# One Trainium2 core, two transformer blocks: input projection with gate and rope pairs in turn, rope and weight sums on VectorE, new order of products and of the attention steps

## What is computed

```python
q, k, v, u, b, c, ga, gc = split(hx @ w_in)     # 1024+256+256+1024+1024+1024+1024+1024 columns
q, k = rope(q, cos, sin), rope(k, cos, sin)     # x*cos + rotate_half(x)*sin
y = b * conv3(c * u)                            # three taps along the tokens
o = window_attention(q, k, v, k_ctx, v_ctx, sink)   # 16 heads of 64, 4 key heads, 128-token query blocks
x = x + g1 * ((sigmoid(ga) * (o @ w_proj_attn) + sigmoid(gc) * (y @ w_proj_conv)) @ w_out)
```

## Time and profile before

| | us |
|---|---|
| median of 3 runs (2946.32 to 2947.89) | 2946.53 |
| the profiled execution | 2949.81 |
| its span, first to last instruction | 2948.0 |
| TensorE busy in it | 2778.3 |
| VectorE busy in it | 2023.5 |

### The profile page before, as it was taken

One profiled execution on the slowest core, in us unless ns is written; L12 is line 12 of the kernel. 1 busy time (PEld: TensorE's weight loads), 2 busy tenths in 40 slices (PEclk: granted clock), 3 DMA queues, 4 the chain that ended last, 5 costly groups with the idle time before them and its releaser, 6 DMA issues.

```text
span 2948.0 us, 35284 instructions
## 1 busy us (share of the span) xinstructions
PE 2778.3 (94%) x13692; PEld 2208.9 (75%) x13692; DVE 2023.5 (69%) x2811; ACT 1303.2 (44%) x2017; POOL 724.1 (25%) x607
## 2 busy tenths in 40 slices
PE   7999999999999999898999989999999489999997
PEld 6777777888778778777888866666688378888885
DVE  5344535888875678796666656666645769999997
ACT  4344433333333455322223344444423357777775
POOL 0001202654554012565444411111100301000000
PEclk9999999999999999999999989999999789999998
DMA  4110131445653995132223551010344579999996
GB/s 153 41 44 30 44 107 72 123 132 152 186 150 130 341 264 184 44 89 82 70 73 125 200 190 36 29 36 29 111 155 172 228 265 394 391 396 398 396 397 243
DMA packets 270554, 494.12 MB, mean 168 GB/s; under 512 B 30060, under 2 KB 141828, under 8 KB 269876
## 3 DMA queue, kind: packets, MB, share of 16 engines
q1 hardware_dynamic: 240800, 396.40, 38.5%
q0 software_dynamic: 29440, 95.43, 9.9%
q10 hardware_dynamic: 148, 0.04, 0.0%
HBM read 424.60 MB, written 67.21 MB: 167 GB/s over the span
## 4 chain that ended last, share of the span: by engine, by line
PE 76%; DVE 12%; ACT 4%; issue 3%; DMA 3%; POOL 1%; SPq 0%; POOLq 0%; DVEq 0%; ACTq 0%
PE PS L131 72%; DVE m L140 6%; PE PS L134 5%; ACT m L137 4%; DVE m L149 2%; DMA m<-in_w_down_dram 1%; DVE m L146 1%; POOL m L140 1%; DVE small L143 1%; DVE m L176 0%; DVE m L182 0%; DMA m<-x_scratch 0%; DVE m L185 0%; DVE m L179 0%; SPq L188 0%
## 5 line engine op out<-in xcount | busy, mean ns | idle before, releaser
L131 PE MATMUL PS<-m,m 128*128 128x512 f32 (+6 forms) x11818 | 2567.7, 391 | 66.2 <-DVE m L140 37.9
L131 PEld LDWEIGHTS PS<-m,m 128*128 128x128 f32 (+2 forms) x11818 | 1998.7, 186 | 565.4 <-issue 111.1
L137 ACT ACTIVATE m<-m 128x512 fp32r<-128x512 f32 (+5 forms) x893 | 810.8, 929 | 942.5 <-PE PS L131 526.2
L140 DVE TENSOR_TENSOR m<-m,m 128x512 fp32r<-128x512 f32 (+5 forms) x860 | 1027.3, 1225 | 179.2 <-ACT m L137 153.8
L140 POOL TENSOR_TENSOR m<-m,m 128x512 f32<-128x512 f32 (+3 forms) x236 | 366.8, 1558 | 604.4 <-DVE m L140 232.8
L140 DVE TENSOR_TENSOR m<-PS,m 128x512 f32<-128x512 f32 (+1 forms) x456 | 300.4, 683 | 302.7 <-PE PS L131 260.1
L137 ACT ACTIVATE m<-PS 128x512 f32<-128x512 f32 (+3 forms) x481 | 267.1, 579 | 365.6 <-PE PS L131 171.4
L134 PE MATMUL PS<-ident,m 128*128 128x128 f32 x1650 | 236.6, 284 | 82.5 <-DVE m L155 37.7
L134 PEld LDWEIGHTS PS<-ident,m 128*128 128x128 f32 x1650 | 198.8, 146 | 133.5 <-DVE m L155 38.3
L137 ACT ACTIVATE m<-m,small 128x640 f32<-128x640 f32 (+4 forms) x200 | 157.1, 788 | 262.7 <-DVE small L143 195.6
L149 DVE CUSTOM_DVE_ANT_0 m<-PS,m 128x640 f32<-128x640 f32 (+4 forms) x192 | 146.3, 775 | 143.5 <-PE PS L131 143.4
(11 more groups left out here) (88 smaller groups left out, 484.1 us busy)
## 6 DMA issues: line engine op xcount, KB each, us to landing
m<-in_w_exp_gate_dram SPq DMA_DIRECT2D x64, 1024.0 KB, 8.4
m<-in_w_exp_up_dram SPq DMA_DIRECT2D x64, 1024.0 KB, 8.7
m<-in_w_exp_down_dram SPq DMA_DIRECT2D x64, 1024.0 KB, 8.5
m<-in_w_mod_dram SPq DMA_DIRECT2D x48, 512.0 KB, 3.7
m<-in_w_gate_up_dram SPq DMA_DIRECT2D x44, 512.0 KB, 6.5
m<-in_w_in_dram SPq DMA_DIRECT2D x21, 1024.0 KB, 5.4
m<-in_w_in_dram SPq DMA_DIRECT2D x25, 512.0 KB, 5.1
x_scratch<-m POOLq DMA_DIRECT2D x24, 512.0 KB, 2.9
```

What stands on the lines that cost most here:

```text
L131: return Unsent() if self.e is None else self.e.matmul(o, l, r, start=first, stop=last, **k)
L137: return Unsent() if self.e is None else self.e.activation(o, i, fn, **k)
L140: return Unsent() if self.e is None else self.e.tensor_tensor(o, a, b, op)
```

## The change

In words: (1) `ST` is reordered: g and rope pairs alternate for the first nine, the last four g pairs stay at the end. (2) `ST_ORDER` becomes P1 P6 P7 P5 P2 P4 P3. (3) From the second pair on VectorE makes S1 to S4. (4) Rope is done by VectorE alone, quarter by quarter, in two buffers. (5) The residual's loads and products move to the last three pairs, and the load of k (`k2`) behind them and behind the y loads. (6) In the transposes' stage low parts come earlier in VectorE's list, and sums of the first pair later in GpSimd's. (7) In the attention part p goes to step p+1 (two parts at step 59), `values2` of a group follows the first half part of the next step, ScalarE copies the first chunk out ahead of the exponentials, y is split over 8 steps, and the first two blocks of the convolution's projection are split in the last pair. (8) The split of the attention's output starts when part 63 is done.

```diff
+        ST = [("g", 0), ("k", 0), ("g", 1), ("q", 0), ("g", 2), ("q", 1), ("g", 3), ("q", 2), ("q", 3)] + [
+            p for j in range(4) for p in (("b", j), ("u", 2 * j), ("u", 2 * j + 1))] + [("g", j) for j in range(4, 8)]
...
-        ST = [("k", 0)] + [("q", c) for c in range(4)] + [
-            p for j in range(4) for p in (("b", j), ("u", 2 * j), ("u", 2 * j + 1))] + [("g", j) for j in range(8)]
         NST = len(ST)
         LAST = NST - 1
         C_AT = {ST[c]: c for c in range(NST)}
-        ST_ORDER = "P1 P6 P2 P7 P5 P4 P3".split()
+        ST_ORDER = "P1 P6 P7 P5 P2 P4 P3".split()
+        ROPE_C = [C_AT["k", 0]] + [C_AT["q", j] for j in range(4)]
+        ROPE_Q = ["22", "11", "21", "12"]
         ST_B = {"P1": "B11", "P2": "B21", "P3": "B22", "P4": "T4", "P5": "T1", "P6": "T2", "P7": "T3"}
...
-        gt = [ar(68 + 2 * n, 512) for n in range(4)]
-        xr, growb = [ar(144, 1024), ar(152, 1024)], ar(148, 1024)
...
+        gt_early = [piece(44, 512, F32), piece(46, 512, F32), ar(152, 512), ar(154, 512)]
+        gt_late = [ar(68 + 2 * n, 512) for n in range(4)]
+        xr, growb = [piece(44, 1024, F32), ar(152, 1024)], ar(148, 1024)
...
-        def st_sums(pool, c):
-            if c == NST:
+        def st_sums(e, c):
+            if c == NST or e.name != ("DVE" if c else "POOL"):
...
+            dve.tensor_tensor(a, a, cosT[:, cs], ALU.mult).then_inc(*dve.did("rope_cos", n))
+            dve.tensor_tensor(b_, b_, sinT[:, cs], ALU.mult).then_inc(*dve.did("rope_sin", n))
             dve.wait_ge("rope_sin", n)
             dve.tensor_tensor(a, a, b_, ALU.add).then_inc(*dve.did("rope_out", n))
...
+            for c in range(2, LAST):
                 w_load(sp, W_ST + c)
-                if 20 <= c < 24:
-                    residual_load(sp, 2 * c - 40)
-                    residual_load(sp, 2 * c - 39)
+            residual_load(sp, 0)
+            residual_load(sp, 1)
+            w_load(sp, W_ST + LAST)
+            residual_load(sp, 2)
+            residual_load(sp, 3)
             w_load(sp, W_PC)
-            sp.wait_ge("x2n_st0", 6)
-            sp.wait_ge("x2n_st1", 7)
-            for n in range(17, 20):
-                sp.wait_ge(f"rope_st{n % 3}", n)
-            sp.dma_start(k2, q_dram[1024:1280, :].rearrange("(k p) n -> p k n", p=128)).then_inc(*sp.landed("k_in"))
+            residual_load(sp, 4)
+            residual_load(sp, 5)
             w_load(sp, W_PC + 1)
+            residual_load(sp, 6)
+            residual_load(sp, 7)
+            for n in range(18, 20):
+                sp.wait_ge(f"rope_st{n % 2}", n)
             sp.wait_ge("st_acc", LAST, "P6")
-            for i in range(4):
-                q_load(sp, i)
+            q_load(sp, 0)
             sp.wait_ge("y_st0", 6)
             sp.wait_ge("st_acc", LAST, "P7")
             y_load(sp, 0)
             sp.wait_ge("st_acc", LAST, "P5")
             y_load(sp, 1)
+            sp.wait_ge("x2_last", 7)
+            sp.dma_start(k2, q_dram[1024:1280, :].rearrange("(k p) n -> p k n", p=128)).then_inc(*sp.landed("k_in"))
+            for i in range(1, 4):
+                q_load(sp, i)
             sp.wait_ge("st_acc", LAST, "P4")
             for i in range(4, NT):
                 q_load(sp, i)
...
             st_product(pe, 0, "P1")
-            st_product(pe, 0, "P2")
             st_product(pe, 0, "P5")
-            pe.kept = (bank_of["st_acc", 0, "P5"],)
+            pe.kept = (bank_of["st_acc", 0, "P1"], bank_of["st_acc", 0, "P5"])
             for i in range(4):
                 turn_tn(pe, "T2", i)
+            st_product(pe, 0, "P2")
             st_product(pe, 0, "P7")
-            pe.kept += (bank_of["st_acc", 0, "P7"],)
...
-                kind, j = ST[c]
                 if kind == "g":
-                    for q in ("22", "21", "12"):
-                        gate_sigmoid(act, j, q)
+                    gate_sigmoid(act, j, "22")
+                st_c11(act, c)
+                if c == LAST:
+                    w_high(act, W_PC + 1)
+                st_high(act, c + 1, "P2")
+                st_high(act, c + 1, "P4")
+                if kind == "g":
+                    gate_sigmoid(act, j, "21")
+                    gate_sigmoid(act, j, "12")
...
-                st_u2(dve, c)
-                rope_join(dve, 4 * c - 1)
+                resid = range(3 * (c - LAST + 2), min(8, 3 * (c - LAST + 3))) if c > LAST - 3 else ()
+                st_low(dve, c, "P3")
+                rope(dve, c - 1, "12")
                 st_low(dve, c + 1, "P1")
-                st_low(dve, c + 1, "P6")
                 for m in taps:
                     conv_taps(dve, m, 0)
                     conv_taps(dve, m, 1)
-                st_low(dve, c + 1, "P2")
-                if kind == "g" and 1 <= j <= 4:
-                    residual_norm(dve, 2 * j - 2)
-                    residual_norm(dve, 2 * j - 1)
+                st_u2(dve, c)
+                st_sums(dve, c + 1)
+                st_low(dve, c + 1, "P6")
+                for i in resid[:1]:
+                    residual_norm(dve, i)
                 st_u3(dve, c)
-                rope_turn(dve, 4 * c)
                 for m in taps:
                     conv_taps(dve, m, 2)
                     conv_taps(dve, m, 3)
                 st_low(dve, c + 1, "P7")
+                if c == LAST:
+                    w_low(dve, W_PC)
                 st_c22(dve, c)
-                rope_join(dve, 4 * c)
-                if c < 5:
-                    rope_turn(dve, 4 * c + 1)
+                rope(dve, c, "22")
                 st_low(dve, c + 1, "P5")
+                for i in resid[1:2]:
+                    residual_norm(dve, i)
+                rope(dve, c, "11")
+                st_low(dve, c + 1, "P2")
+                if c == LAST:
+                    w_low(dve, W_PC + 1)
                 st_c21(dve, c)
-                if c < 5:
-                    rope_join(dve, 4 * c + 1)
-                    rope_turn(dve, 4 * c + 2)
+                rope(dve, c, "21")
+                for i in resid[2:3]:
+                    residual_norm(dve, i)
                 st_low(dve, c + 1, "P4")
                 st_c12(dve, c)
-                if c < 5:
-                    rope_turn(dve, 4 * c + 3)
-                    rope_join(dve, 4 * c + 2)
-                st_low(dve, c + 1, "P3")
 
         def second_pool(pool):
             for i in (4, 5, 6):
                 modulate_pool(pool, i)
             for i in range(4):
                 x2_store(pool, i)
...
-        FILL0, NFILL = 3, 64
+        NFILL = 64
+        FILL = {s: [s - 1] if s < 59 else [58, 59] if s == 59 else [s] for s in range(1, 64)}
+        FILL_END = {p // 4: s for s in FILL for p in FILL[s] if p % 4 == 3}
...
-            if s < 2:
-                return [(0, 4 * s + k) for k in range(4)]
-            return [(1, 2 * s - 4 + k) for k in range(2)] if s < 6 else []
+            return [(n // 8, n % 8) for n in (2 * s, 2 * s + 1)] if s < 8 else []
...
+                halves = [(p, k1) for p in FILL.get(s, []) for k1 in range(2)]
                 if s + 1 < NS2:
                     qk2(pe, s + 1)
-                fill_part(pe, s - FILL0, 0)
+                for p, k1 in halves[:len(halves) // 2]:
+                    fill_part(pe, p, k1)
+                if s and j == 0:
+                    values2(pe, s // 4 - 1)
                 turn2(pe, s, 0)
                 turn2(pe, s, 1)
-                fill_part(pe, s - FILL0, 1)
+                for p, k1 in halves[len(halves) // 2:]:
+                    fill_part(pe, p, k1)
                 if len(chunks2(s)) == 3:
                     turn2(pe, s, 2)
                 if s > 4 and j == 1:
                     sums2(pe, s // 4 - 1)
-                if j == 3:
-                    values2(pe, s // 4)
-            for p in range(NS2 - FILL0, NFILL):
-                fill_part(pe, p, 0)
-                fill_part(pe, p, 1)
...
-                exp2(act, s + 1, 0)
+                if s == 0:
+                    exp2(act, 1, 0)
+                    exp2(act, 1, 1)
                 p2_evacuate(act, s, 0)
-                exp2(act, s + 1, 1)
+                if s:
+                    exp2(act, s + 1, 0)
+                    exp2(act, s + 1, 1)
...
-                if s > 4 and s % 4 == 2:
-                    pc_take(dve, s // 4 - 1)
-            pc_take(dve, 15)
-            o2_normed(dve, 15)
+                for n in range(16):
+                    if FILL_END[n] == s:
+                        pc_take(dve, n)
...
-            act.wait_ge("o2_sums", 15)
+            act.wait_ge("pc_acc", 15)
...
-            dve.wait_ge("pc_st0")
-            dve.wait_ge("pc_st1")
             for h in range(2):
                 if h:
                     w_low(dve, W_PA + 1)
                 for k in range(8):
+                    if h == 0 and k == 2:
+                        dve.wait_ge("o2_acc", 15)
+                        dve.wait_ge("s2_acc", 63)
+                    if h == 0 and k == 4:
```

(27 more changed lines are left out.)

242 lines of the change are left out of this document (126 added, 116 removed).

## The result

The changed kernel takes 2894.93 us (median of 4 runs, 2891.19 to 2896.51) against 2947.21 for the kernel before: ratio 0.9821, 95% interval 0.9804 to 0.9838. It is 52 us faster; 2886 was forecast, with a range of 2868 to 2910. The profiled execution took 2895.70 us, its span is 2893.6.

A forecast was written before the change was run, and what follows sets the result against it. VectorE was taken to bound the rope pairs, stalling TensorE. Gains 27.6 + 5.3 + 1.2 + 2.5 + 19 + 5 = 60.6 us from 2949.8 gave 2889.2, less 3.3 for the median: 2886, range 2868 to 2910.

The forecast's parts named there:

- VectorE's price: Pair stage: a 512-element VectorE operation costs 0.60 us with GpSimd not multiplying; 0.935 was the other bound.
- 1.2 beside GpSimd: Pair stage: a VectorE operation costs 1.2 us while GpSimd runs its products.
- C22 before P3: Pair stage: P3, starting 16.3 us into a pair, waits for C22, so VectorE's list order counts.
- 28.8: Pair stage: gain from rope loss taken back, 27.6 us, and from the residual's vanished wait, 1.2 us.
- 1.7 of clock: After a TensorE stall: the lower granted clock costs another 1.7 us.
- The transposes: Stage ahead of the pairs: earlier low parts remove the 3.20 us stall and its clock, shrink another; +5.3 us.
- +2.5: Start of the attention: shorter first steps outweigh the later arrival of k, a net gain of 2.5 us.
- 8 to 11: Hand-over to the attention: first scores start 8 to 11 us behind the products, waiting for k; 0.88 before.
- step period: First attention steps: about 4.4 us each in place of 5.9, so step 5 after 26 to 28 us.
- Rival (b): Hand-over to the attention costs more: k lands at 35 rather than 28, clock stays low; 12 us less, 2898; chance 0.12.
- Steady attention: Attention steps: PSUM-bank waits before third chunk and product with v vanish; +19 us, from 13.4 to 22.
- The end: End of the attention: the output's split hides under the last product with v and the sum; +5 us.

The follow-up runs named there:

- rope_gp: Changed kernel with the product of rope's shuffled half by sin back on GpSimd; ratio 0.9851 to the kernel before.
- sums_pool: Changed kernel with the sums S1 to S4 of every pair back on GpSimd; ratio 0.9824 to the kernel before.
- order_old: Changed kernel with the earlier order of products, P1 P6 P2 P7 P5 P4 P3; ratio 0.9882 to the kernel before.
- rope_row: Changed kernel with the five rope pairs in a row instead of alternating with g pairs; ratio 0.9828 to the kernel before.
- k_sink_y: Changed kernel with half of k loaded early, sink values loaded two pairs earlier, y split one step ahead; ratio 0.9775 to the kernel before.
- k_half: Changed kernel with half of k loaded early, right behind weight block W_PC; ratio 0.9775 to the kernel before.
- the two runs: Changed kernel with the product with v back at each group's end: alone, ratio 0.9818; with ScalarE's copy also back between exponentials, 0.9869 to the kernel before.

## Why the prediction was right, point by point

The median lies in the range and near the forecast, and most terms of the sum came out; one did not, the start of the attention, and others hid a part of it.

**VectorE's price: right.** In the pair stage the operations last 0.69 us and start 0.60 apart, with GpSimd silent in g and rope pairs. The group whose mean was 0.935 before, from 1240 to 1410 of the changed kernel:

```profile
L140 DVE TENSOR_TENSOR m<-m,m 128x512 fp32r<-128x512 f32 x66 | 45.0, 685 | 14.7 <-ACT m L137 14.7
```

The marks inside the pairs answer the forecast well. VectorE's timeline in the g pair that began at 1297.69, from U2 to the low part behind C22:

```profile
1305.70 0.68 DVE L140 TENSOR_TENSOR m<-PS,m 128x512 f32<-128x512 f32 x1
...
1309.43 0.68 DVE L140 TENSOR_TENSOR m<-PS,m 128x512 f32<-128x512 f32 x1
1310.03 0.68 DVE L140 TENSOR_TENSOR m<-m,m 128x512 fp32r<-128x512 f32 x1
1310.63 0.69 DVE L140 TENSOR_TENSOR m<-PS,m 128x512 f32<-128x512 f32 x1
1311.23 0.68 DVE L140 TENSOR_TENSOR m<-m,m 128x512 fp32r<-128x512 f32 x1
```

U2 starts at 8.0 and C22 at 12.9 into the pair; 8 to 9 and 13.7 to 14.5 were forecast. Read in the same way, C22 starts at 16.4 in pair 2 (16.6 to 17.4 forecast, the one stall: 0.68 of "up to 1") and at 14.1 behind u pairs (14.9). Only behind the two rope pairs in a row it was worse than I took it: 15.8, and P3 started 0.2 late.

**What the "1.2 beside GpSimd" was: a wrong reading of a right row.** The earlier trace rows has two operations in 2.38 us, and I took half of it as the price of each. GpSimd beside them, in the kernel before:

```profile
1275.98 1.78 POOL L140 TENSOR_TENSOR m<-m,m 128x512 f32<-128x512 f32 x1 [1.96 <-DVE m L176]
```

Its product ended at 1277.76; the pair of operations ended at 1275.93 + 2.38 = 1278.31, half a microsecond later. The first took its 0.69 as ever, and the second, of 1.77, was held until GpSimd was done. In rope_gp, where one operation of VectorE at a time meets a product, VectorE's mean stays at 0.691 and GpSimd pays, with 1.787 (in sums_pool a sum of the same size that meets no operation of VectorE takes 1.28 to 1.29). That only one of the two goes on at a time agrees with what the Trainium skill (SBUF, "Who interferes with whom") says of the lock between them.

**Which wait set the pair stage: partly wrong.** I wrote that what counts is C22 before P3. With VectorE's new lists there is a second deadline that I did not name, the copy of P1 before P2 behind a rope pair's C12; order_old puts it at 18.5 us, the largest of the four parts undone one by one. The others are worth 12.1 (rope's product), 3.4 (g and rope in turn) and 3.3 (sums). They are not additive: 37 us stand against 30 gained. That the sum came out right (30.0 for 28.8) rests on the new order meeting both deadlines; as to the second, which I had not seen, that was luck. No run undoes the move of the residual.

**A stall does not always cost 1.7 of clock.** I added this for each stall. In rope_row stalls of up to 1.53 us cost nothing more; in rope_gp 7.1 us of added waits, in two long stalls, cost 12.1. In order_old 12.4 us of added waits cost 18.5: three of its six stalls are followed by the lower level, and of two equal stalls of 2.04 us one is followed by the lower level (mean of 0.58 in its 4 us) and one is not:

```profile
1312.00:1316.00 4.00, 3.83 (x10) 3.00 (x11) 3.93 (x8) 0.64 (x2) 0.54 (x1) 0.58 0.79 259
...
1354.00:1358.00 4.00, 3.81 (x17) 3.14 (x18) 3.93 (x8) 0.65 (x2) 0.54 (x1) 1.00 0.85 198
```

**The transposes: 8.7 for 5.3.** No wait above 0.3 us is left; the one of 1.75, of which I took 0.4, went entirely, and so did two of 0.35 and 0.69 that I had left out. With the 3.20 these waits are 6.0 us, with the 1.7 of clock 7.7 of the 8.7. This is read from the two traces; no run undoes this part.

**The start of the attention: the step that failed, by 13 us.** "+2.5" was -10.3 (-12.3 and +2.0), and two of its terms were mis-sized. The first is the "8 to 11": TensorE's first scores came 12.86 us behind the last product, 1.9 to 4.9 more. k's load took 18.1 us from issue to landing (the longest of the q_scratch loads),

```profile
DMA to landing us min/median/max: 6.3/11.9/18.1
```

and y's 14.3 and 18.3. They were issued when I had said, 8.3, 11.1 and 13.9 us into the last pair, and landed at 22.6, 29.4 and 32.0, where I had 16.8, 23.4 and 27 to 30. The first y is what I took too short: 8.6 us, though its row stood at 11.9.

The larger error is the step period. I took 4.4 us and 26 to 28 from the first scores to the transposes of step 5; it was 1746.17 - 1710.88 = 35.3. TensorE's timeline in the changed kernel, the last three of these transposes and the waits between them:

```profile
1731.74 1.03 PE L134 MATMUL PS<-ident,m 128*128 128x128 f32 x8
...
1735.67 4.56 PE L131 MATMUL PS<-m,m 128*128 128x512 f32 x19 [1.14 <-DVE m L140]
1740.16 1.09 PE L134 MATMUL PS<-ident,m 128*128 128x128 f32 x8
...
1745.36 0.97 PE L131 MATMUL PS<-m,m 128*128 128x512 f32 x3 [2.34 <-DVE m L140]
1746.17 1.03 PE L134 MATMUL PS<-ident,m 128*128 128x128 f32 x8
```

From the scores to the first transposes it took 6.0 us, at the lower clock level; then the steps took 5.4, 4.7, 4.8, 8.4 and 6.0: 29.3, where five steps of 4.4 are 22.0. A plain step is thus only 0.3 longer than 4.4: the part that TensorE multiplies in a step needs the y of just the step before, and behind it maximum and exponential are nearly as long a ring (k_sink_y). Most of the error lies in what a mean period left out: the clock behind the stall, the product with v in the fourth step (16 of the 19 matmuls) and the accumulator's hand-over in the fifth, whose wait is 2.34 us where the others are 1.14. k_half shows that k's place alone was worth 12.3, paid back in part until the sink values move as well.

Rival (b) has the size (12.3 + 9.1 - 8.6, so 12.8 against its 12), but its mechanism came true in part: k landed at 32.0, not 35, and the clock was back at its upper level from 1722 on (mean 1.00 from 1722 to 1733), so the rest is the steps.

**Steady attention and end: right in sum.** 19.2 for 19. By the two runs the copy's place is 15.2 of it, above my upper bound of 14, and the product's 4.3, below my lower bound of 6.8: two errors that cancel. The end gave 5.7 for 5, with the clock full at the projection; no run undoes this part.

Too low in transposes, pairs and end by 5.3 together, too high by 13 at the start: the net is the 7 us between 60.6 and 53.3. The median missed by 8.9, a little more, since the profiled execution of the kernel before stood 3.3 above its median, and that of the changed kernel 0.8.

## What to carry to other kernels

Where several engines feed one, list every deadline of a pair (each product's input, its bank, the buffer of the copy behind it), not only the one that stalls today: a new list moves the binding one. At the border of two stages look through the queue for every load that the first step needs, the smallest too; when the first is early, the next is late, and here it was one of 16 values. And count a step's period as the longest ring through it, not as the sum of what was taken out, and add what comes once a group: here a product and the hand-over of a bank.

## What was not expected of the hardware

A wait of 0.16 us for a PSUM bank costs 0.33 us each (15.2 us for 46), twice what the waits view shows, while one of 0.56 ahead of the product with v costs 0.36 (4.3 us for 12). Two equal stalls of 2.04 us of TensorE were followed once by the 1.2 GHz level and once not. And over 13 traces the stages of one core repeat within 0.1 us where the code is the same, but for the one that waits for a transfer (0.9), while what lies ahead of the region differs by up to 5.8 us and what follows the last matmul by 2.8: most of the scatter between kernels lies outside the code that was changed.
